# The root of the mixer's RMS norm, applied behind the input projections instead of in front of them

## The chip, the cores and the metric

One core of one Trainium2 chip runs the whole program. TensorE (PE) multiplies, VectorE (DVE), ScalarE (ACT) and GpSimd (Pool) do the elementwise work, and SyncE (SP) fetches weights. The metric is the device time of one execution in microseconds, as the median of several runs. Everything is float32: each matrix product is done as three products of split operands (high times high, low times high, high times low), so each activation tile needs a high part and a low part before PE can use it.

## The reference, cut to what matters

Two blocks run one after the other on 1024 tokens of width 1024. The first block ends in a layer norm. The second block begins with the lines below; what comes after them (the output projection, the feed-forward part, the gated embedding) is not touched.

```python
x = _layernorm(DN_ALPHA * x + y, ssd_ln_g, ssd_ln_b)      # end of the first block
h = x
a = rmsnorm(h, g_mix)                  # h * rsqrt(mean(h*h) + 1e-6) * g_mix
proj = a @ w_in
cb, cc, cu, q, k, v = split(proj)      # 512 columns each
v_ = cc * cu; y = causal 3-tap conv(v_) per channel; conv = cb * y; conv_out = head_rmsnorm(conv)
z = q . k * dh**-0.5                   # 8 heads of 64, stick-breaking attention
a_ij = exp(log_sigmoid(z_ij) + sum of log_sigmoid(-z) over the keys between j and i)
attn = a @ v; attn_out = head_rmsnorm(attn)
h = h + concat(conv_out, attn_out) @ w_out
```

The norm's root is one number per token. `a @ w_in` is linear, so the root of a token can be multiplied in behind the product.

## The kernel before, in words

Activations lie with the channels on the partitions: `H` is eight tiles k of 128 channels by 1024 tokens, `XH` and `XL` are the high and low parts of the eight tiles that the projections read. A weight slab is 128 output columns by all 1024 input channels; PE does it in eight pieces k, one for each tile, of six matmuls of 512 columns. SP fetches slabs into `w_stage`; Pool splits each into `w_hi` and `w_lo` (`split`, L612 and L615: one cast and four subtractions). `next_slab(n)` waits until slab n - 2 is done on PE, because two slots are there. A sum over the channels is a matmul with a matrix of ones (`CN`).

Each engine is one queue in program order, and its order is written out by hand; semaphores join the queues. Around the change the program runs as follows.

- PE does pieces of a small projection (`proj_piece`, L1243) between the norms' sums. `norm_sums` (L1036) adds up eight square tiles with 16 matmuls, once for the layer norm (`ln2`) and once for the mixer norm (`mix`). ACT makes the squares into two buffers `SQN` and waits for PE to have read the one before last.
- For the layer norm DVE makes `TN = H * gain * root` (L2531) and `H = TN + bias` (L2523) for the eight tiles, while ACT squares `TN + bias` (L1976). With the sums of these ACT makes the mixer's root. DVE then goes over the tiles a second time: `TN = H * g_mix * root` (L2531), ACT copies it to `XH` (L1762), and DVE makes `XL = TN - XH` (L2519).
- The input projection has 24 slabs in the order `SB_ORDER`: v0, q0, k0, cc0, cu0, v1, q1, k1, cb0, cc1, ... , cb3, in four rounds m of 128 channels (two heads). PE does the first two slabs interleaved: eight pieces of slab 0 with pieces of slab 1 between them, as tiles become ready (`mix["lo"]`). Then comes slab k0, the turning of v, and the attention.
- The attention goes in 12 steps a round, of up to 128 keys by 512 queries for two heads, over 10 blocks of keys in flight behind each other. `SB_FILL` sets how many pieces of later slabs PE does in each step. In a step PE makes scores (L1315), DVE copies them to `ZS` (L2874), ACT makes abs, exp and ln of it (L2060, L2072, L2074), DVE makes the softplus (L2905), ACT its high part (L2084), DVE its low part (L2907), PE the suffix sums (L1332), DVE subtracts them (L2889), ACT makes the weight (L2079) and its high part `WH` (L2089), DVE its low part `WL` (L2845), and PE multiplies with v (L1354).
- The convolution's channels go beside it: ACT copies cc into `CC` (L2008), DVE multiplies cu in (L2809), applies the three taps into `CONV` (L2822, L2825) and multiplies cb in (L2813).

## Time and profile before

| | |
|---|---|
| median of 3 runs | 2723.09 us (2722.91 to 2728.45) |
| the profiled execution | 2722.69 us, its span 2720.9 us |
| PE busy | 2642.7 us, 97% of the span |
| DVE, ACT, Pool busy | 1713.4, 938.1, 1150.4 us |
| granted PE clock | full in all 40 slices |
| first layer-norm tile scaled | at 1372.74 us |
| slabs 0 and 1 (v0, q0) done on PE | at about 1421.8 us |
| attention | 1436 to 1864 us |

Times are counted from the start of the span. A row of the timeline is: start, length, engine, line, operation, what is written from what is read, count, and in brackets how long the engine had been idle and what ended that. A matmul of 512 columns is shown with a modelled end, so its row is longer than its share of PE's time; the distance of two starts is the better measure. A row of the groups is: line, engine, operation, operands and sizes, count, then busy time, mean in ns, idle time before and its releasers. A row of a stretch is: its length, then busy time and count of PE, of the weight loads, of DVE, ACT and Pool, the granted clock, the share of the DMA engines and GB/s.

### The profile page before, as it was taken

To read this page: it belongs to the slowest core of one execution; us is meant where nothing else is said; L and a number is where in the kernel's file an instruction comes from. 1 tells how busy PE (TensorE), PEld (TensorE's weight loads), DVE (VectorE), ACT (ScalarE), POOL (GpSimd) and SP (SyncE) were. 2 spreads that over 40 slices of the span, in tenths; PEclk is the share of its full clock that TensorE was granted. 3 is DMA by queue.
4 is the path that set the end of the run, shared out by engine and by line. 5 is a ranking of instruction groups with operands and counts; after the bars stand their busy time and mean duration, and the time that the engine had idled before them with its cause. 6 is when DMAs were issued, how large, how long until landed. Compare 5 with 4: busy or idle time off the path is not lost.

```text
span 2720.9 us, 32191 instructions
## 1 busy us (share of the span) xinstructions
PE 2642.7 (97%) x12394; PEld 2117.3 (78%) x12394; DVE 1713.4 (63%) x2087; ACT 938.1 (34%) x1208; POOL 1150.4 (42%) x1422
## 2 busy tenths in 40 slices
PE   8999999999999999999999999998999999999998
PEld 7877878787887887887767777776888888888886
DVE  6636663778658658758865665666355656555556
ACT  2537880422212211212256666575211111111132
POOL 4633435431431431431421222223555676655653
PEclk9999999999999999999999999999999999999999
DMA  3110003210110110110230000002111111111312
GB/s 135 51 47 32 24 20 109 66 47 24 39 48 23 40 54 16 47 47 16 78 131 24 32 24 32 24 32 85 55 39 55 55 55 55 47 47 54 117 47 78
DMA packets 39937, 139.37 MB, mean 51 GB/s; under 512 B 4400, under 2 KB 4528, under 8 KB 39792
## 3 DMA queue, kind: packets, MB, share of 16 engines
q1 hardware_dynamic: 31392, 110.11, 12.3%
q10 hardware_dynamic: 8400, 27.26, 2.7%
q8 instruction: 99, 1.62, 0.3%
q14 instruction: 46, 0.38, 0.0%
HBM read 124.77 MB, written 12.58 MB: 50 GB/s over the span
## 4 chain that ended last, share of the span: by engine, by line
PE 82%; DVE 11%; ACT 4%; issue 2%; POOL 1%; ACTq 0%; DVEq 0%; POOLq 0%
PE PS L759 37%; PE PS L1437 13%; PE PS L1463 10%; PE PS L996 2%; PE PS L1089 2%; PE PS L1485 2%; PE PS L1130 2%; PE PS L1315 1%; PE PS L895 1%; PE PS L1332 1%; PE PS L909 1%; PE PS L1354 1%; PE PS L1132 1%; PE PS L1036 1%; ACT mla_p L1662 1%
## 5 line engine op out<-in xcount | busy, mean ns | idle before, releaser
L612 POOL CAST w_hi<-w_stage 128x1024 fp32r<-128x1024 f32 x130 | 143.3, 1102 | 1116.7 <-PE PS L759 757.9
L615 POOL TENSOR_TENSOR w_lo<-w_stage,w_hi 128x256 fp32r<-128x256 f32 x520 | 504.2, 1000 | 10.4
L759 PE MATMUL PS<-XH,w_hi 128*128 128x512 f32 x1216 | 384.6, 398 | 7.7 <-DVE XL L2519 2.9
L759 PE MATMUL PS<-XL,w_hi 128*128 128x512 f32 x1216 | 375.9, 390 | 0.0
L759 PE MATMUL PS<-XH,w_lo 128*128 128x512 f32 x1216 | 375.4, 390 | 0.0
L759 PEld LDWEIGHTS PS<-XH,w_hi 128*128 128x128 f32 x1216 | 222.4, 188 | 61.0 <-issue 10.0
L759 PEld LDWEIGHTS PS<-XL,w_hi 128*128 128x128 f32 x1216 | 228.4, 188 | 48.5
L759 PEld LDWEIGHTS PS<-XH,w_lo 128*128 128x128 f32 x1216 | 228.4, 188 | 48.4
L686 POOL TENSOR_TENSOR w_lo<-w_stage,w_hi 128x256 fp32r<-128x256 f32 x260 | 220.3, 854 | 0.0
L682 POOL CAST w_hi<-w_stage 128x256 fp32r<-128x256 f32 x260 | 125.9, 487 | 185.7 <-PE PS L1437 108.3
L1437 PE MATMUL PS<-raw_hi,w_hi 128*128 128x512 f32 x512 | 158.2, 390 | 0.0
L1437 PE MATMUL PS<-raw_hi,w_lo 128*128 128x512 f32 x512 | 157.8, 390 | 0.0
L1437 PE MATMUL PS<-raw_lo,w_hi 128*128 128x512 f32 x512 | 157.8, 389 | 0.0
L1463 PE MATMUL PS<-ffn_u_hi,w_lo 128*128 128x512 f32 x392 | 152.7, 390 | 0.0
L1463 PE MATMUL PS<-ffn_u_hi,w_hi 128*128 128x512 f32 x392 | 152.7, 390 | 0.0
L1463 PE MATMUL PS<-ffn_u_lo,w_hi 128*128 128x512 f32 x392 | 152.7, 389 | 0.0
L3009 DVE TENSOR_TENSOR H<-H,PS 128x512 f32<-128x512 f32 x140 | 96.0, 686 | 77.0 <-PE PS L1463 77.0
L2950 DVE SCALAR_TENSOR_TENSOR ffn_t<-PS,root 128x1024 f32<-128x1024 f32 x32 | 39.2, 1225 | 154.3 <-PE PS L1437 145.1
L2139 ACT ACTIVATE ffn_t<-ffn_t 128x1024 f32<-128x1024 f32 x32 | 34.0, 1061 | 240.0 <-DVE ffn_t L2950 240.0
L1437 PEld LDWEIGHTS PS<-raw_hi,w_hi 128*128 128x128 f32 x512 | 96.2, 188 | 20.2 <-issue 0.5
L1437 PEld LDWEIGHTS PS<-raw_lo,w_hi 128*128 128x128 f32 x512 | 96.2, 188 | 19.9
L1437 PEld LDWEIGHTS PS<-raw_hi,w_lo 128*128 128x128 f32 x512 | 96.2, 188 | 19.9
(459 smaller groups left out, 5620.7 us busy)
## 6 DMA issues: line engine op xcount, KB each, us to landing
w_stage<-w SPq DMA_DIRECT2D x202, 512.0 KB, 3.3
H<-x_t ACTq DMA_DIRECT2D x8, 512.0 KB, 8.0
pj_kept<-ple_proj_tiles ACTq DMA_DIRECT2D x8, 512.0 KB, 2.6
h_kept<-H ACTq DMA_DIRECT2D x8, 512.0 KB, 3.5
H<-h_kept ACTq DMA_DIRECT2D x4, 1024.0 KB, 5.0
out_t<-out_tiles SPq DMA_DIRECT2D x16, 256.0 KB, 2.1
x_again<-x_t ACTq DMA_DIRECT2D x12, 256.0 KB, 3.1
ple_proj_a<-pj_kept ACTq DMA_DIRECT2D x1, 2048.0 KB, 9.1
```

Source lines behind the costliest of these rows:

```text
L612: nc.gpsimd.tensor_copy(w_hi[:, slot, :, :], w_stage[:, slot, :, :]).then_inc(s_w_hi, 1)
L615: nc.gpsimd.tensor_tensor(w_lo[:, slot, k:k + 2, :], w_stage[:, slot, k:k + 2, :], w_hi[:, slot, k:k + 2, :].bitcast(F32), ALU.subtract).t ...
L682: nc.gpsimd.tensor_copy(ring(w_hi, e), src).then_inc(s_eh.sem, 1)
L686: nc.gpsimd.tensor_tensor(ring(w_lo, e), src, ring(w_hi, e).bitcast(F32), ALU.subtract).then_inc(done, count)
L759: mm = nc.tensor.matmul(outs[:, half, :], wt[:, slot, k, :], a[:, k - first, half * HB:(half + 1) * HB], start=(k == whole[0] and wt is w_ ...
L996: mm = nc.tensor.matmul(PS[:, 2 * (n % 2) + half, :], wt[:, n % 2, k, :], a[:, k, half_cols(half)], start=(k == 0 and wt is w_hi and a is ...
L1089: mm = nc.tensor.matmul(PS[:, half, :], wt[:, n % 2, k, :], a[:, k, half * HB:(half + 1) * HB], start=(k == 0 and wt is w_hi and a is XH), ...
L1130: nc.tensor.matmul(PS[:, 2, 64 * h:64 * h + 64], E[:, c % 2, h, :], XF[:, c % 2, 64 * h:64 * h + 64], start=True, stop=True)
L1437: mm = nc.tensor.matmul(PS[:, 2 * (c % 2) + half, :], ring(wt, e + k // 2, k % 2), a[:, k, half * HB:(half + 1) * HB], start=(k == 0 and w ...
L1463: mm = nc.tensor.matmul(PS[:, BANK[j], :], ring(wt, e + i, k), a[:, ACTS_AT[j], k, :], start=(j not in BEFORE and k == 0 and wt is w_hi an ...
L1485: mm = nc.tensor.matmul(PS[:, 4 + 2 * e + half, :], ring(wt, e0 + k // 2, k % 2), a[:, t, half * HB:(half + 1) * HB], start=(first and wt ...
L3009: v.tensor_tensor(dst, dst, src, ALU.add).then_inc(s_dr, 1)
```

## The change

What is done to the mixer norm:

- `XH` and `XL` are made from `H * g_mix`, with no root in them. `norm_two` takes the place of two calls of `norm_dve`: one pass in which DVE makes `TN`, then `H` (a tile later), then `XL` (two tiles later), and ACT makes the square and `XH` of each tile and issues the copy of `H` to `h_kept` behind it.
- PE's 16 matmuls over the squares are gone. The squares go into four buffers; Pool adds the first four tiles (`mix_add`, three additions around the split of slab 1), DVE the last four behind the last `XL`, and PE does two matmuls with ones over the sum, in the middle of slab k0.
- ACT makes the root `RM` (one number a token, on all partitions) while PE does the rest of k0. DVE makes from it `RK`, the same numbers with the tokens on the partitions (`key_roots`).
- The root comes in at four places. The score copy is `PS * RK * RM` (key's root and query's root). The weights' high and low parts are multiplied by `RK` (the root of v's token). Pool multiplies `CC` by `RM * RM` (cc and cu have one root each) and `CONV` by `RM` (for cb).
- PE's order of slabs 0 and 1 is `MIX_PIECES`: 0 0 0 1 1 0 1 0 1 0 1 0 1 0 1 1.

The diff, cut to its core:

```diff
+MIX_PIECES = [0, 0, 0, 1, 1, 0, 1, 0, 1, 0, 1, 0, 1, 0, 1, 1]
...
+            def mix_add(k):
+                mix["sq"].wait(pool, k + 1)
+                if k > 1:
+                    mix["ss"].wait(pool, k - 1)
+                nc.gpsimd.tensor_tensor(ACM[:, :], mix_square_at(0) if k == 1 else ACM[:, :], mix_square_at(k), ALU.add).then_inc(mix["ss"].sem, 1)
+            def root_squared():
+                mix["rs"].wait(pool, 1)
+                nc.gpsimd.tensor_tensor(RM2[:, :], RM[:, :], RM[:, :], ALU.mult).then_inc(mix["c"].sem, 1)
+            def gate_rooted(m):
+                pool.wait_ge(s_bank, sb_bank_turn(("cc", m)) + 1)
+                mix["c"].wait(pool, root_product("cc", m) - 1)
+                nc.gpsimd.tensor_tensor(CC[:, :], CC[:, :], RM2[:, :], ALU.mult).then_inc(mix["c"].sem, 1)
+            def taps_rooted(m):
+                pool.wait_ge(s_cc, cc_step("tap", m, 2))
+                nc.gpsimd.tensor_tensor(CONV[:, m, :], CONV[:, m, :], RM[:, :], ALU.mult).then_inc(mix["c"].sem, 1)
+            mix_add(1)
+            next_slab(N_IN2 + 1)
+            mix_add(2)
+            mix_add(3)
+            for i in range(2, len(SB_ORDER)):
+                next_slab(N_IN2 + i)
+                if i == 5:
+                    root_squared()
+                if SB_ORDER[i - 2][0] == "cc":
+                    gate_rooted(SB_ORDER[i - 2][1])
+                if SB_ORDER[i][0] == "cb" and i < len(SB_ORDER) - 1:
+                    taps_rooted(SB_ORDER[i][1])
+            next_slab(N_OUT2)
+            taps_rooted(3)
+            next_slab(N_OUT2 + 1)
...
-            norm_sums(mix)
...
+            for i in MIX_PIECES:
+                sb_piece(i, done[i])
+                done[i] += 1
+            progress[0] = 16
+            sb_pieces(4)
+            mix["ss"].wait(pe, KT - 1)
+            for half in range(2):
+                mm = nc.tensor.matmul(PS[:, 2 + half, :], CN[:, C_ONES, :], ACM[:, half * HB:(half + 1) * HB], start=True, stop=True)
+            mm.then_inc(mix["cs"].sem, 1)
+            sb_pieces(4)
...
-                        nc.scalar.activation(WH[:, T1 % 2, :, q1:HB], a, ACT.Copy).then_inc(s_wh, 1)
+                        nc.scalar.activation(WH[:, T1 % 2, :, q1:HB], a, ACT.Copy, scale=RK[:, j1:j1 + 1]).then_inc(s_wh, 1)
...
-            norm_dve(ln2, "ln2_g", center=centre2, split=False, keep=True)
-            norm_dve(mix, "g_mix")
+            norm_two(centre2)
...
-                v.tensor_tensor(WL[:, T % 3, :, q0:HB], ZS[:, T % 3, :, q0:HB], WH[:, T % 2, :, q0:HB].bitcast(F32),
-                                ALU.subtract).then_inc(s_wl, 1)
+                v.scalar_tensor_tensor(out=WL[:, T % 3, :, q0:HB], in0=ZS[:, T % 3, :, q0:HB], scalar=RK[:, j:j + 1],
+                                       in1=WH[:, T % 2, :, q0:HB].bitcast(F32), op0=ALU.mult, op1=ALU.subtract).then_inc(s_wl, 1)
...
-                        v.tensor_copy(z, PS[:, 0:2, q0:HB]).then_inc(s_zc, 1)
+                        v.scalar_tensor_tensor(out=z, in0=PS[:, 0:2, q0:HB], scalar=RK[:, j:j + 1],
+                                               in1=RM[:, hf * HB + q0:(hf + 1) * HB].unsqueeze(1).to_broadcast([P, 2, HB - q0]),
+                                               op0=ALU.mult, op1=ALU.mult).then_inc(s_zc, 1)
```

DVE's queue between the layer norm's last tiles and the end of the tile work. Before (L2531 scales, L2523 adds the bias, L2519 makes `XL`):

```order
L2531 SCALAR_TENSOR_TENSOR norm_t<-H,VC,norm_rs 128x1024
L2523 TENSOR_SCALAR H<-norm_t,VC 128x1024 x2
L2531 SCALAR_TENSOR_TENSOR norm_t<-H,VC,norm_rs 128x1024 x2
L2519 TENSOR_TENSOR XL<-norm_t,XH 128x1024
L2531 SCALAR_TENSOR_TENSOR norm_t<-H,VC,norm_rs 128x1024
```

Now (L2599 scales, L2593 adds the bias, L2588 makes `XL`, L2611 adds squares):

```order
L2599 SCALAR_TENSOR_TENSOR norm_t<-H,VC,norm_rs 128x1024
L2593 TENSOR_SCALAR H<-norm_t,VC 128x1024
L2588 SCALAR_TENSOR_TENSOR XL<-H,VC,XH 128x1024
L2593 TENSOR_SCALAR H<-norm_t,VC 128x1024
L2588 SCALAR_TENSOR_TENSOR XL<-H,VC,XH 128x1024 x2
L2611 TENSOR_TENSOR mix_square_sum<-mix_square_sum,norm_sq 128x1024 x2
L2611 TENSOR_TENSOR mix_square_sum<-mix_square_sum,mix_sq_b 128x1024 x2
```

The second pass over the tiles is gone, `XL` stands between the layer norm's own steps, and four additions stand behind the last `XL`.

Pool's queue around the split of slab 1 (the second cast of each piece). Before:

```order
L612 CAST w_hi<-w_stage 128x1024
L615 TENSOR_TENSOR w_lo<-w_stage,w_hi 128x256 x4
L612 CAST w_hi<-w_stage 128x1024
L615 TENSOR_TENSOR w_lo<-w_stage,w_hi 128x256 x4
L612 CAST w_hi<-w_stage 128x1024
```

Now:

```order
L649 TENSOR_TENSOR w_lo<-w_stage,w_hi 128x256 x4
L697 TENSOR_TENSOR mix_square_sum<-norm_sq 128x1024
L646 CAST w_hi<-w_stage 128x1024
L649 TENSOR_TENSOR w_lo<-w_stage,w_hi 128x256 x4
L697 TENSOR_TENSOR mix_square_sum<-mix_square_sum,mix_sq_b 128x1024 x2
L646 CAST w_hi<-w_stage 128x1024
```

One addition stands ahead of the split of slab 1 and two behind it, ahead of the split of k0.

Pool's queue at the split of slab v1 (the sixth of the input projection), where the first products with the root stand. Before there were casts and subtractions alone, as above; now:

```order
L649 TENSOR_TENSOR w_lo<-w_stage,w_hi 128x256 x4
L646 CAST w_hi<-w_stage 128x1024
L649 TENSOR_TENSOR w_lo<-w_stage,w_hi 128x256 x4
L701 TENSOR_TENSOR mix_root_squared<-mix_root 128x1024
L706 TENSOR_TENSOR conv_gated<-conv_gated,mix_root_squared 128x1024
L646 CAST w_hi<-w_stage 128x1024
```

Three more gates (L706) and four products of the taps (L710) follow in the same manner, each alone behind the split of a slab.

## Rows read from the trace of the kernel before

**Rows 1.** The page, busy time of each engine:

```profile
PE 2642.7 (97%) x12394; PEld 2117.3 (78%) x12394; DVE 1713.4 (63%) x2087; ACT 938.1 (34%) x1208; POOL 1150.4 (42%) x1422
```

**Rows 2.** Busy time by stretch: the mixer's squares, and slab 0's start:

```profile
1380.20:1390.20 10.00, 9.95 (x23) 4.45 (x24) 8.46 (x9) 6.57 (x6) 0.00 (x0) 1.00 0.84 337
...
1396.80:1403.70 6.90, 4.64 (x18) 3.23 (x18) 6.87 (x4) 4.09 (x4) 6.82 (x5) 1.00 0.38 152
```

**Rows 3.** Timeline of PE: the mixer's sums, slab 0's second piece, slab k0's first:

```profile
1380.25 10.57 PE L1036 MATMUL PS<-norm_sq,CN 128*128 128x512 f32 x24 [0.54 <-ACT norm_sq L1976]
...
1400.43 0.74 PE L759 MATMUL PS<-XH,w_hi 128*128 128x512 f32 x2 [1.93 <-DVE XL L2519]
...
1421.83 0.73 PE L759 MATMUL PS<-XH,w_hi 128*128 128x512 f32 x2
```

**Rows 4.** The chain that ended last, slabs 0 to 2:

```profile
1403.78 29.23 PE PS L759 x126
```

**Rows 5.** Groups of instructions from 1369.8 to 1421.8 us, PE, DVE and ACT:

```profile
L1036 PE MATMUL PS<-norm_sq,CN 128*128 128x512 f32 x34 | 15.5, 599 | 0.6 <-ACT norm_sq L1976 0.5
...
L2523 DVE TENSOR_SCALAR H<-norm_t,VC 128x1024 f32<-128x1024 f32 x8 | 5.9, 748 | 0.0
...
L1976 ACT ACTIVATE norm_sq<-norm_t,VC 128x1024 f32<-128x1024 f32 x8 | 9.1, 1148 | 5.1 <-PE PS L1036 2.2 <-DVE norm_t L2531 2.0 <-ACT ple_proj_tiles L1954 0.9
...
L1954 ACT ACTIVATE ple_proj_tiles<-PS 128x1024 f32<-128x1024 f32 x4 | 4.0, 1006 | 0.0
```

**Rows 6.** Timeline of DVE: scaling without Pool beside it, a split with it:

```profile
1372.74 2.48 DVE L2531 SCALAR_TENSOR_TENSOR norm_t<-H,VC,norm_rs 128x1024 f32<-128x1024 f32 x2 [8.97 <-ACT norm_rs L1542]
...
1382.28 1.28 DVE L2531 SCALAR_TENSOR_TENSOR norm_t<-H,VC,norm_rs 128x1024 f32<-128x1024 f32 x1
...
1398.64 1.74 DVE L2519 TENSOR_TENSOR XL<-norm_t,XH 128x1024 fp32r<-128x1024 f32 x1
```

**Rows 7.** Timeline of Pool: the splits of slabs 1 and 2:

```profile
1396.34 1.30 POOL L612 CAST w_hi<-w_stage 128x1024 fp32r<-128x1024 f32 x1 [31.98 <-PE PS L1243]
1397.72 6.60 POOL L615 TENSOR_TENSOR w_lo<-w_stage,w_hi 128x256 fp32r<-128x256 f32 x4
1417.83 1.04 POOL L612 CAST w_hi<-w_stage 128x1024 fp32r<-128x1024 f32 x1 [13.52 <-PE PS L759]
1418.95 2.83 POOL L615 TENSOR_TENSOR w_lo<-w_stage,w_hi 128x256 fp32r<-128x256 f32 x4
```

**Rows 8.** Groups of instructions of Pool, all: its operation on 1024 columns:

```profile
L633 POOL TENSOR_TENSOR XL<-H,XH 128x1024 fp32r<-128x1024 f32 x7 | 16.5, 2370 | 0.0
```

**Rows 9.** Groups by shape, the replaced operations (in the attention) and their like:

```profile
L2874 DVE COPY sb_z<-PS 128x1024 f32<-128x1024 f32 x24 | 29.2, 1218 | 0.1
...
L2551 DVE SCALAR_TENSOR_TENSOR ssd_conv<-PS,VC,ssd_conv 128x1023 f32<-128x1023 f32 x24 | 30.8, 1283 | 0.8
...
L2089 ACT ACTIVATE sb_weight_hi<-sb_z 128x1024 fp32r<-128x1024 f32 x24 | 25.1, 1046 | 0.1
...
L1915 ACT ACTIVATE ssd_y_hi<-ssd_conv,VC 128x1024 fp32r<-128x1024 f32 x12 | 13.8, 1154 | 11.9 <-DVE ssd_conv L2690 11.9
```

**Rows 10.** Waits, 1436 to 1863 us (waiter, releaser, total us, times, longest):

```profile
PEld PS L1354 <- DVE sb_weight_lo L2845: 15.7, 24, 2.0
...
PEld PS L1332 <- DVE sb_softplus_lo L2907: 9.8, 10, 1.5
```

**Rows 11.** Timeline of Pool, DVE and PE at slab cb0's split:

```profile
1519.29 3.87 POOL L615 TENSOR_TENSOR w_lo<-w_stage,w_hi 128x256 fp32r<-128x256 f32 x4
...
1523.69 1.23 DVE L2907 TENSOR_TENSOR sb_softplus_lo<-sb_softplus,sb_softplus_hi 128x1024 fp32r<-128x1024 f32 x1 [1.13 <-ACT sb_softplus_hi L2084]
...
1524.97 0.74 PE L1332 MATMUL PS<-sb_softplus_hi,from_r 128*128 128x512 f32 x2 [0.68 <-DVE sb_softplus_lo L2907]
```

**Rows 12.** Timeline of Pool and DVE at the end of the attention:

```profile
1854.79 1.64 POOL L612 CAST w_hi<-w_stage 128x1024 fp32r<-128x1024 f32 x1 [25.86 <-PE PS L759]
...
1855.45 2.06 DVE L2845 TENSOR_TENSOR sb_weight_lo<-sb_z,sb_weight_hi 128x1024 fp32r<-128x1024 f32 x1
```

## What the change does to the time, predicted from these rows

> **What bounds the kernel now.** I read the page first. PE is busy for 97% of the span [rows 1], so time is won only where PE waits or does work that can go. The busy time by stretch and PE's timeline show where that is around the mixer's norm. The 16 matmuls of its sums stand in the trace as two rows each; 24 rows take 10.57 us, or 0.44 each [rows 3], so the sums alone take PE 14 us, in which it is full and DVE is busy for 8.46 of 10 us [rows 2]. When slab 0 begins, PE is busy for 4.64 us of 6.9, since DVE makes each `XL` out of two steps and shares its time with Pool [rows 2]; PE's longest wait there is 1.93 us [rows 3]. Behind that, PE runs without a gap: 126 matmuls in 29.23 us, or 1.39 us for a piece of six [rows 4]. Slab k0 starts at 1421.83 us [rows 3]. That moment is the gauge of the first half of the change. The second half lies in the attention, where PE's weight loads wait for the weights' low part in 24 of 48 steps and for the softplus' low part in 10 [rows 10]. So there DVE is the late one in up to half of the steps, and what is added to it costs something.
>
> The sum is made against the profiled execution of 2722.7 us; the median, 2723.1, is 0.4 more.
>
> **The norm's stretch: when does k0 start?** Up to the first scaled tile at 1372.74 us nothing changes [rows 6]. From there DVE has for each tile a scaling of 1.28 us, a bias step of 0.75 and an `XL` of about 1.28 (it now has a gain too, like the scaling) [rows 5, 6]: 3.31 us, and 26.5 for eight. Alone it would have the last `XL` at 1399.2. ACT has less to do: eight squares of 1.15, eight `XH` of 1.15 (an ACT copy with a gain takes that [rows 9]) and four copies of 1.01 are 22.4 us [rows 5]; it sets no end.
>
> Pool lies beside this with the split of slab 1 and three additions. What a Pool operation costs DVE can be read in one place for a short one: beside Pool's quarters of the split an `XL` took 1.74 us instead of some 1.25 [rows 6], so a quarter costs 0.5. Pool pays too: the split took 1.30 and 6.60 us with DVE beside it and 1.04 and 2.83 alone [rows 7]. For a cast on 1024 columns it is more: it began at 1854.79 and lasted 1.64, and the DVE subtraction that began at 1855.45 behind it took 2.06 us, 0.84 too long [rows 12]. It looks as if each waits for the other to end. The slab's split then costs DVE 0.7 + 4 x 0.5 = 2.7 us. An addition on 1024 columns takes Pool 2.37 us [rows 8]; no row shows one beside a DVE operation that reads two tiles of SBUF. Its price is between 0.45, as for a quarter, and 2.1, nearly its whole length. I take 1.5, since the cast is nearest in size and held DVE for most of its own length: 4.5 us for three. The last `XL` is then at 1399.2 + 2.7 + 4.5 = 1406.4.
>
> The Trainium skill (SBUF — State Buffer, section on SBUF's two separate sides) states that the loser of the pair of ports that VectorE and GpSimd share "fully blocks", for the whole instruction, when the VectorE instruction has two SBUF inputs. Rows 12 agree for a cast; no row shows a two-input Pool operation of 2.37 us. By that rule an addition here would cost about 2.1, by the rule of the short row 0.45; the first would move the whole sum to slower, the second to faster, and each is a rival below.
>
> PE needs eight pieces of slab 0 and eight of slab 1, and has a few waiting when the last `XL` comes; I put the end of slab 0 at 1409. Only then may Pool split k0. DVE's four additions (4.9 us at 1.22) run then, so the split takes some 5 us, between 3.9 alone and 7.9 [rows 7], where before it was hidden behind slab 1. k0 starts at 1414: **7.8 us earlier**. PE idles for 2 us before it; the two pieces of slab 1 left are no cover for the split. The bounds are 1410 (additions at 0.45, last `XL` at 1403.3) and 1416 (at 2.1, last `XL` at 1408.2, and PE, starved on the way, ends slab 0 at 1411.5).
>
> **The two matmuls over the sum** are four such rows of 0.44 us: **+1.8**. The 16 that go give PE nothing of their own here: DVE's walk above sets k0's start, and it has left them out. The squares are all added by then. The root's logarithm and exponential, `key_roots` on DVE and one more table load run beside the second half of k0, 5.5 us, and its turning; they cost nothing unless the root is over 3 us late. The copies to `h_kept` and the projection's last pieces move with ACT and are not waited for.
>
> **Arithmetic in the attention.** The score copy goes from 1.218 to 1.283 us, what DVE takes from PSUM with a tile and a column [rows 9]; the weights' low part gains a column too, +0.06; its high part on ACT goes from 1.046 to 1.154 [rows 9]. That is 0.23 us a step. If all 48 steps paid it, it would be 11 us; if only the 24 that wait for the weights paid, and half of them absorbed it in the order of the queues, some 1.5. Lower bound nothing. I take **+1.5**: the chain that ended last goes through PE in most of the attention.
>
> **Pool's nine products in the attention.** The split of cb0 ends at 1523.16; the softplus' low part starts at 1523.69, and PE already waits for it 0.68 us [rows 11]. The product for y starts between the two and takes 2.37 [rows 8], so it can hold DVE for up to 1.85, straight onto PE. The same pattern stands in rounds 1 and 2. At slab cc0 two products follow each other in steps that wait for DVE: up to 2. At the end of the last round the last product starts with the taps, and the split and the cast chain of rows 12 move behind it: up to 1.5. The gates of cc1 to cc3 fall where PE has 18 matmuls to go on with; I cost them nothing, and up to 1 together where that cover is short. At most that makes 3 x 1.85 + 2 + 1.5 + 1 = 10; at 0.45 apiece, five on the path, 2.3. I take 1.2 for each of the three, 1.2 and 0.7: **+5.5**. cu and cb wait for Pool's products too, but these are done a slab earlier, except cb3's, which ends at about the time its slab does.
>
> **Sum:** -7.8 + 1.8 + 1.5 + 5.5 = +1.0, so 2723.7 against the profiled execution and 2724.1 against the median. I forecast **2724.1 us**, no change that can be measured.
>
> **Rivals.**
>
> - *Pool's long operations cost DVE no more than short ones.* k0 starts at 1410, -11.8; +1.8, +1.5, +2.3: -6.2, or 2716.9. For it: nothing in the trace shows a long hold by a two-input operation. Against it: the cast of rows 12.
> - *Each Pool operation holds DVE for its whole length* (the rule above). k0 starts at 1416, -5.8; +1.8, +1.5, +10: +7.5, or 2730.6. It decides from a hold of about 1.9 us where PE already waits for the softplus' low part. For it: rows 11 and 12. Against it: Pool may start just after DVE, and then Pool is the one that waits.
> - *The attention is covered by PE's slabs*: neither the arithmetic nor the products reach PE, and only the norm's gain is left, -7.8 + 1.8 = -6.0, or 2717.1. Against it: 34 waits of rows 10.
> - *The longer steps of the attention all reach PE*: -7.8 + 1.8 + 11 + 5.5 = +10.5, or 2733.6. Against it: the chain goes mostly through PE.
>
> **How the numbers follow.** The forecast's own range is 2718 to 2728.5, with a chance of 0.50. The first rival gets 0.16, the third 0.09, the second 0.18 and the fourth 0.07. A difference of 0.2%, 5.4 us, is about what a measurement of this kernel can tell from no change. Faster by more: the two faster cases, 0.25, and 0.02 out of the forecast's tail; slower by more: the two slower ones, 0.25; the rest, 0.48. The range that should hold it 8 times in 10 reaches over both signs: 2713 to 2733. It leaves out the faster cases' better halves and what lies beyond the fourth rival's lower half.
>
> **What would show each step.** In the profile after: the start of the first matmul of k0 (1410, 1414 or 1416); the time of the last `XL` and the length of a DVE step beside a Pool addition (1.7 or 3.3); the idle time of PE before k0, by Pool's `w_lo`; the length of the score copy (1.28) and of `WH` (1.15); and in the attention the length of the softplus' low part in the step behind each product for y (1.23, or up to 3.1), with PE's wait behind it. From k0's start to the end of the attention (1864) 442 us pass before; the forecast adds 9 to it. More than 13 added would make it wrong on the slow side, less than 4 on the fast side.

## The result, and the profile after

| | before | after |
|---|---|---|
| median | 2725.43 us (6 runs, 2722.91 to 2730.12) | 2735.75 us (6 runs, 2734.27 to 2737.16) |
| ratio | | 1.0037, 95% interval 1.0027 to 1.0047 |
| profiled execution, its span | 2722.69, 2720.9 us | 2734.27, 2732.4 us |
| mean granted clock of it | 0.998 | 0.993 |

The change makes the kernel 10.3 us slower. The forecast was 2724.1 with a range to 2733; the time lies above both.

Busy times of the page after, to set beside [rows 1]: PE has no more work than before, and it is idle for 90.9 us of its span where it was idle for 78.2.

```profile
PE 2641.5 (97%) x12366; PEld 2116.9 (77%) x12366; DVE 1737.2 (64%) x2085; ACT 942.4 (34%) x1208; POOL 1181.1 (43%) x1434
```

The first scaled tile comes at 1372.74 us in the trace of before and at 1373.95 in the trace after; in the other kernels' traces it lies anywhere from 1372.4 to 1377.9, in code that is the same in all. So all offsets below are counted from that first scaled tile: `k0` is the start of slab k0, `att` the first scores, `end` the last head sums, each against the same moment of before (49.1, 63.8 and 497.8 us after the first scaled tile).

| after, against before | k0 | att | step 4 | round 1 | round 2 | round 3 | end |
|---|---|---|---|---|---|---|---|
| us | -6.3 | -3.0 | -0.3 | +1.6 | +5.3 | +7.9 | +10.1 |

**The norm's stretch.** DVE's timeline of after, then Pool's. Two scalings that fall beside a Pool addition take 3.42 and 3.38 us where they take 1.28 alone, and a bias step (0.75 in [rows 5]) takes 2.89.

```profile
1380.19 3.42 DVE L2599 SCALAR_TENSOR_TENSOR norm_t<-H,VC,norm_rs 128x1024 f32<-128x1024 f32 x1
...
1391.14 3.38 DVE L2599 SCALAR_TENSOR_TENSOR norm_t<-H,VC,norm_rs 128x1024 f32<-128x1024 f32 x1
1394.44 2.89 DVE L2593 TENSOR_SCALAR H<-norm_t,VC 128x1024 f32<-128x1024 f32 x1
...
1406.75 1.28 DVE L2588 SCALAR_TENSOR_TENSOR XL<-H,VC,XH 128x1024 fp32r<-128x1024 f32 x1 [0.25 <-ACT XH L2054]
```

```profile
1379.49 3.04 POOL L697 TENSOR_TENSOR mix_square_sum<-norm_sq 128x1024 f32<-128x1024 f32 x1 [13.92 <-ACT norm_sq L2050]
...
1390.09 6.69 POOL L697 TENSOR_TENSOR mix_square_sum<-mix_square_sum,mix_sq_b 128x1024 f32<-128x1024 f32 x2
1411.90 1.04 POOL L646 CAST w_hi<-w_stage 128x1024 fp32r<-128x1024 f32 x1 [15.12 <-PE PS L828]
1413.02 3.64 POOL L649 TENSOR_TENSOR w_lo<-w_stage,w_hi 128x256 fp32r<-128x256 f32 x4
```

PE's timeline of after, in slab 0 and at the start of k0, and the stretches around them (the granted clock is the third number from the end of a row of a stretch). Two matmuls of a product start 0.45 us before the next two at full clock (the forecast's 1.39 us for six); here they are 0.85 apart, and the granted clock is 0.72 and 0.79, where it was 1.00 throughout before. Between its two levels, 2.4 and 1.2 GHz, PE ran at the lower one for a few us, each time behind a wait of about 2 us.

```profile
1391.27 1.22 PE L828 MATMUL PS<-XH,w_hi 128*128 128x512 f32 x2 [1.96 <-DVE XL L2588]
1392.29 1.06 PE L828 MATMUL PS<-XL,w_hi 128*128 128x512 f32 x2
1393.14 1.06 PE L828 MATMUL PS<-XH,w_lo 128*128 128x512 f32 x2
...
1416.72 0.73 PE L828 MATMUL PS<-XH,w_hi 128*128 128x512 f32 x2 [2.17 <-POOL w_lo L649]
...
1418.37 1.06 PE L828 MATMUL PS<-XH,w_hi 128*128 128x512 f32 x2
1419.22 1.06 PE L828 MATMUL PS<-XL,w_hi 128*128 128x512 f32 x2
...
1423.94 1.88 PE L1452 MATMUL PS<-mix_square_sum,CN 128*128 128x512 f32 x4
```

```profile
1383.20:1395.40 12.20, 8.21 (x25) 5.78 (x24) 12.20 (x8) 5.40 (x6) 11.71 (x7) 0.72 0.59 217
...
1416.70:1424.70 8.00, 7.98 (x26) 6.16 (x27) 0.28 (x1) 0.21 (x1) 3.73 (x5) 0.79 0.40 131
```

**The attention.** The place of [rows 11], now with the product of the taps in it: the softplus' low part takes 2.88 us where it took 1.23, and PE waits 2.34 us for it where it waited 0.68. A round later a wait of 2.33 us at the same step is followed by pairs 0.85 to 1.02 us apart, so at the lower clock. It is the only one of the three such waits (2.34, 2.33 and 2.33 us, in rounds 0 to 2) at which the clock fell.

```profile
1524.24 2.37 POOL L710 TENSOR_TENSOR conv_out<-conv_out,mix_root 128x1024 f32<-128x1024 f32 x1
...
1524.81 2.88 DVE L3000 TENSOR_TENSOR sb_softplus_lo<-sb_softplus,sb_softplus_hi 128x1024 fp32r<-128x1024 f32 x1 [1.13 <-ACT sb_softplus_hi L2156]
...
1527.75 0.74 PE L1400 MATMUL PS<-sb_softplus_hi,from_r 128*128 128x512 f32 x2 [2.34 <-DVE sb_softplus_lo L3000]
...
1643.41 1.22 PE L1400 MATMUL PS<-sb_softplus_hi,from_r 128*128 128x512 f32 x2 [2.33 <-DVE sb_softplus_lo L3000]
1644.43 1.05 PE L1400 MATMUL PS<-sb_softplus_lo,from_r 128*128 128x512 f32 x2
```

The groups by shape and the waits of the attention in the trace after answer to [rows 9] and [rows 10]. The longer steps have the forecast's sizes; the wait for the softplus' low part has grown from 9.8 us in 10 waits to 15.5 in 9, that for the weights' from 15.7 to 20.4.

```profile
L2965 DVE SCALAR_TENSOR_TENSOR sb_z<-PS,SM,mix_root 128x1024 f32<-128x1024 f32 x24 | 30.7, 1278 | 0.1
L2162 ACT ACTIVATE sb_weight_hi<-sb_z,SM 128x1024 fp32r<-128x1024 f32 x24 | 27.3, 1139 | 0.1
```

```profile
PEld PS L1422 <- DVE sb_weight_lo L2934: 20.4, 24, 2.1
PEld PS L1400 <- DVE sb_softplus_lo L3000: 15.5, 9, 2.8
```

### The profile page after: what moved, and what is told of

Same layout as the page of the kernel before. It is cut to its first block, busy times and chain, and to the rows that moved or that the text cites. A ratio compares the mean times of both kernels' runs of the same rounds, so it can differ in the third digit from the quotient of the medians.

```text
span 2732.4 us, 32159 instructions
## 1 busy us (share of the span) xinstructions
PE 2641.5 (97%) x12366; PEld 2116.9 (77%) x12366; DVE 1737.2 (64%) x2085; ACT 942.4 (34%) x1208; POOL 1181.1 (43%) x1434
## 4 chain that ended last, share of the span: by engine, by line
PE 79%; DVE 13%; ACT 4%; issue 3%; POOL 1%; ACTq 0%; DVEq 0%; POOLq 0%
PE PS L828 35%; PE PS L1511 13%; PE PS L1537 10%; PE PS L1065 2%; PE PS L1158 2%; PE PS L1559 2%; PE PS L1199 2%; PE PS L964 1%; PE PS L978 1%; PE PS L1383 1%; PE PS L1201 1%; PE PS L1422 1%; PE PS L1400 1%; DVE ssd_x L2685 1%; ACT mla_p L1736 1%
## 5 line engine op out<-in xcount | busy, mean ns | idle before, releaser
L1511 PEld LDWEIGHTS PS<-raw_hi,w_hi 128*128 128x128 f32 x512 | 96.1, 188 | 20.4 <-issue 0.5
```

What stands on the lines that cost most here:

```text
L1511: mm = nc.tensor.matmul(PS[:, 2 * (c % 2) + half, :], ring(wt, e + k // 2, k % 2), a[:, k, half * HB:(half + 1) * HB], start=(k == 0 and w ...
```

## The experiments

All were run beside the kernel before; its median was 2725.16 us for the first four, 2725.28 for the next four, 2725.09 for the three after them and 2725.85 for the last. The offsets are those of the profiled execution, counted as above. The clock is the mean granted clock of all timed runs of a kernel (before: 0.996). The ratio and its interval are taken over the timed runs and are not the quotient of the two medians; where the runs of a kernel scatter widely, as in f1, e4 and g3, the two differ by up to 0.0009. Runs of one kernel scatter by several us, so a difference of less than about 3 us between two medians is not clear of noise.

| kernel | median, us | ratio to before, 95% | clock | k0 | att | end |
|---|---|---|---|---|---|---|
| the change | 2735.75 | 1.0037 (1.0027 to 1.0047) | 0.9922 | -6.3 | -3.0 | +10.1 |
| e1 tiny products | 2725.68 | 1.0001 (0.9991 to 1.001) | 0.9939 | -6.4 | -3.0 | +2.6 |
| e2 norm alone | 2722.48 | 0.9991 (0.9981 to 1.0) | 0.9940 | -6.3 | -3.0 | -3.4 |
| e3 products in quarters | 2727.92 | 1.0007 (0.9998 to 1.0017) | 0.9938 | -6.4 | -3.0 | +3.4 |
| e4 tiny additions | 2731.79 | 1.0016 (1.0007 to 1.0026) | 0.9924 | -12.7 | -9.4 | +6.8 |
| f1 no y product | 2726.05 | 1.001 (1.0001 to 1.002) | 0.9938 | -6.3 | -3.0 | +3.3 |
| f2 additions on DVE | 2735.63 | 1.0038 (1.0026 to 1.0049) | 0.9919 | -9.3 | -5.9 | +7.7 |
| f3 filler before k0 | 2736.76 | 1.004 (1.0026 to 1.0054) | 0.9910 | -6.4 | -4.7 | +11.0 |
| f4 all on DVE | 2722.47 | 0.9989 (0.9979 to 0.9998) | 0.9942 | -9.3 | -7.6 | -5.7 |
| g1 y product later | 2730.11 | 1.0016 (1.0007 to 1.0025) | 0.9923 | -6.4 | -4.6 | +5.1 |
| g2 v root once | 2725.08 | 0.9996 (0.9987 to 1.0005) | 0.9952 | -9.3 | -5.9 | -2.2 |
| g3 plain scores | 2724.69 | 0.999 (0.9981 to 0.9999) | 0.9946 | -9.3 | -5.9 | +0.4 |
| h1 v root first | 2720.33 | 0.9979 (0.997 to 0.9988) | 0.9948 | -9.0 | -5.6 | -4.4 |

### Which part costs: the products, the arithmetic, the additions

e1 makes Pool's nine products one column wide:

```diff
-                nc.gpsimd.tensor_tensor(CC[:, :], CC[:, :], RM2[:, :], ALU.mult).then_inc(mix["c"].sem, 1)
+                nc.gpsimd.tensor_tensor(CC[:, 0:1], CC[:, 0:1], RM2[:, 0:1], ALU.mult).then_inc(mix["c"].sem, 1)
```

> The changed kernel, but Pool's nine products with the root (its square, four gates of cc, four products of the taps) work on 1 column of 1024, so the convolution's root is left out; all waits stay. Theory H (a long Pool operation holds every DVE operation that reads two tiles of SBUF for its whole length, and PE's clock falls in the gap): of the 12.9 us that the attention lost in the changed kernel some 11 come back, 2735.8 to about 2725, the step behind each split of cb goes back from 2.88 to 1.23 us for the softplus' low part. Theory A (the longer arithmetic, 0.23 us in 48 steps): these products matter little, 2734 or more.

Measured: 2725.68, 10.1 us less than the change. The products cost nearly twice the forecast's 5.5, and they are the whole loss. It is not a kinder clock that did it: in the two profiled executions, between the first scaled tile and the last head sums, the granted clock of e1 is 0.97 and that of the change 0.98, and e1 is still 7.5 us ahead at the end.

e2 does the same and also takes the roots out of the score copy and the weights' two parts, so that only the norm's stretch is changed:

```diff
-                        nc.scalar.activation(WH[:, T1 % 2, :, q1:HB], a, ACT.Copy, scale=RK[:, j1:j1 + 1]).then_inc(s_wh, 1)
+                        nc.scalar.activation(WH[:, T1 % 2, :, q1:HB], a, ACT.Copy).then_inc(s_wh, 1)
```

> As the kernel with one-column products, and the score copy and the weights' high and low parts as in the kernel before, without the root: what is left of the change is the norm's stretch alone. Theory H: at most 1 us less than the kernel with one-column products, and 2 to 4 us faster than the kernel before, since slab k0 starts some 5 us earlier and two matmuls and a stretch at half clock take 3 of them back. Theory A: some 8 us less than with one-column products.

Measured: 2722.48, 2.7 us under before, and 3.2 under e1, which has the arithmetic in addition. Its offset stays at -3.0 us through all 48 steps: what the norm's stretch wins reaches the end, and nothing else is touched.

e3 keeps the products and cuts each into four of 256 columns:

```diff
+                for q in range(4):
+                    s_ = slice(q * P * 2, (q + 1) * P * 2)
+                    ins = nc.gpsimd.tensor_tensor(out_[:, s_], a[:, s_], b[:, s_], ALU.mult)
```

> The changed kernel with each of Pool's nine products as four operations on 256 columns. Theory H: a hold ends with the operation, 0.6 us, and DVE comes in between, so the softplus' low part behind y's product falls from 2.88 to below 2 us; PE's gaps there stay under 1.5 us and its clock stays up: 4 to 6 us faster than the changed kernel. If instead the hold goes by Pool's whole queue, or DVE is slowed by Pool's total work, it is no faster than the changed kernel.

Measured: 2727.92, 7.8 us less than the change with all of the work still there, and more than the 4 to 6 expected. Pool's and DVE's timelines at the place of [rows 11] show why. The low part is not held at all now (1.25 us), the step behind it by 0.5, and Pool takes twice its time: between two quarters DVE gets in.

```profile
1527.29 4.78 POOL L702 TENSOR_TENSOR conv_out<-conv_out,mix_root 128x256 f32<-128x256 f32 x4
...
1527.85 1.25 DVE L3006 TENSOR_TENSOR sb_softplus_lo<-sb_softplus,sb_softplus_hi 128x1024 fp32r<-128x1024 f32 x1 [1.13 <-ACT sb_softplus_hi L2162]
1529.03 1.75 DVE L2940 SCALAR_TENSOR_TENSOR sb_weight_lo<-sb_z,SM,sb_weight_hi 128x1024 fp32r<-128x1024 f32 x1
```

e4 makes the three additions on Pool one column wide instead, and DVE's first one adds the square of tile 4 to itself, so that the squares of tiles 0 to 3 are left out of the sum:

```diff
-nc.gpsimd.tensor_tensor(ACM[:, :], mix_square_at(0) if k == 1 else ACM[:, :], mix_square_at(k), ALU.add).then_inc(mix["ss"].sem, 1)
+nc.gpsimd.tensor_tensor(ACM[:, 0:1], (mix_square_at(0) if k == 1 else ACM[:, :])[:, 0:1], mix_square_at(k)[:, 0:1], ALU.add).then_inc(mix["ss"].sem, 1)
```

> The changed kernel with Pool's three additions of squares on 1 column of 1024, and DVE's first addition from one square twice, so the mean leaves out the first four tiles; waits and DVE's work as before. Theory H: each addition held DVE by about 2 us, so the last XL comes 6 us earlier, slab k0 starts 5 to 7 us earlier and the gaps that lowered PE's clock there shrink: 5 to 7 us faster than the changed kernel. Theory A: no difference.

Measured: k0 starts 6.4 us earlier than in the change, 3 x 2.1, the lengthening of three DVE steps, so the hold is whole there too. But the time falls by 4.0 only: the offset goes from -9.4 at the first scores to -3.4 at the end of round 0. f2, f3 and g1 below lose 3 to 6 us in that round too.

### Is it the place, or the work?

f1 leaves out the four products of the taps (`taps_rooted`) and DVE's wait for them. The head norm divides by the root of the same token again, so only its eps is met otherwise.

```diff
-                if SB_ORDER[i][0] == "cb" and i < len(SB_ORDER) - 1:
-                    taps_rooted(SB_ORDER[i][1])
...
-                    mix["c"].wait(dve, root_product("y", m))
```

> The four products of the taps with the root are left out (the head norm behind them divides by the root of the same token, so only its eps is met otherwise); the root squared and the four gates stay on Pool. The tiny products took 10 us off the changed kernel. Theory H (a Pool operation holds the softplus' low part for its whole length where PE already waits): the y products stand at such places, the gates do not, so leaving four of nine out gives back 6 to 7 of the 10: 2729 (2728 to 2730). Rival N (the products cost by their number, wherever they stand, through DVE's total): four ninths of 10, so 2731.3. By H the softplus' low part behind each y product is back at 1.23 us and PE's wait before it under 1 us.

Measured: 2726.05, 9.7 us less than the change (8.2 by the means of the runs, where e1 has 10.2; 6.8 and 7.5 at the end of the profiled executions). Four of the nine products carry nearly all of the loss that the nine make; with the root squared and the gates gone as well (e1) no further gain is clear of the scatter. Theory H was right about the place and too mild about the size. The trace of f1 still has the 2.7 us of the step at which the root squared and the first gate stand, where e1 has nothing and loses 3.0 us between steps 6 and 10 instead, at and behind the drop of its clock that is shown below.

g1 leaves the product as it is and lets it start 1.8 us or so later, behind the low part that it stood beside:

```diff
             def taps_rooted(m):
                 pool.wait_ge(s_cc, cc_step("tap", m, 2))
+                if m < 3:
+                    pool.wait_ge(s_spl, NU * (m + 1))
```

> The changed kernel with one wait more: in rounds 0 to 2 Pool starts the product of the taps with the root only when DVE has finished the last softplus' low part of the round, beside which it stood; the product itself is the same, and its result is needed some 30 us later. Theory P (the place decides: held is the one step for which PE waits): the jumps of 1.7, 2.9 and 1.8 us at the starts of rounds 1 to 3 go or become small, the low part takes 1.23 us again, and the time is 2730.5 (2729 to 2732). Rival A (a Pool operation of this length costs the same wherever it stands beside DVE): 2735.7.

Measured: 2730.11, 5.6 us less than the change, at the same work and even a lower clock than in e1. The place decides. The jumps at the starts of rounds 1 to 3 are 0.0, 0.0 and 0.1 us (1.7, 2.9 and 1.8 in the change). DVE's and Pool's timelines of g1:

```profile
1528.63 1.23 DVE L3002 TENSOR_TENSOR sb_softplus_lo<-sb_softplus,sb_softplus_hi 128x1024 fp32r<-128x1024 f32 x1 [1.13 <-ACT sb_softplus_hi L2158]
1529.78 1.28 DVE L2936 SCALAR_TENSOR_TENSOR sb_weight_lo<-sb_z,SM,sb_weight_hi 128x1024 fp32r<-128x1024 f32 x1
1531.15 1.22 DVE L2984 TENSOR_TENSOR sb_z<-sb_z,PS 128x1024 f32<-128x1024 f32 x1
...
1530.00 3.31 POOL L712 TENSOR_TENSOR conv_out<-conv_out,mix_root 128x1024 f32<-128x1024 f32 x1 [1.90 <-DVE sb_softplus_lo L3002]
```

DVE has begun the weights' low part 0.22 us before Pool begins, and now Pool is the one that waits: 3.31 us instead of 2.37, DVE 1.28 as ever. And the subtraction behind it, which reads PSUM, runs beside Pool's product in its usual 1.22 us.

The Trainium skill (SBUF — State Buffer, section on SBUF's two separate sides) says just this: of the two the one that starts first has the shared ports for the whole instruction, and it names DVE instructions with two SBUF inputs, and those in a 2-port mode, as the ones concerned. The traces agree for steps with two SBUF tiles (2.88 for 1.23 us), for the free step on PSUM, and for the bias step with one SBUF tile (2.89 for 0.75), if its 0.75 us for 1024 columns is such a mode.

### Where Pool's additions go

f2 lets DVE do the three additions, each behind an `XL`:

```diff
                     if k > 1:
                         low(k - 2)
+                    if 4 <= k <= 6:
+                        squares_added(k - 3)
```

> The three additions of squares that Pool did are done by DVE, one behind each of the XL of tiles 2, 3 and 4 of the one pass; nothing else is changed. By the changed kernel's rows each Pool addition lengthens a DVE step by 2.1 us (3.42 for 1.28, 3.38 for 1.28, 2.89 for 0.75), 6.3 together; three additions on DVE cost 3 x 1.22 = 3.7. Theory H: k0 starts 2.7 us earlier, counted from the first scaled tile, and the time is 2733.1 (2732 to 2734.5). Rival S (k0's start is set by the split of its slab beside DVE's last additions, not by the last XL): no gain, 2735.7. Rival L (the shared time is small): k0 1 us later or more, 2737.

Measured: k0 starts 3.0 us earlier than in the change, as theory H had it (2.7), so rival S is wrong about k0. But the time is 2735.63, no gain. In the profiled execution 2.4 us of the earlier start are left at the end (+7.7 for +10.1); in the timed runs nothing is, at a lower mean clock than any kernel here but f3. The gain is made and given back.

### The clock

f3 puts two matmuls nobody reads into the gap before k0:

```diff
             progress[0] = 16
+            pe.wait_ge(s_pj, 8)
+            for half in range(2):
+                nc.tensor.matmul(PS[:, 2 + half, :], CN[:, C_ONES, :], CN[:, 0:4, :].rearrange("p a t -> p (a t)"), start=True, stop=True)
```

> Two matmuls with ones over constants, whose result nobody reads, stand on PE in the gap of 2.17 us before slab k0 (1.88 us of work); all else is the changed kernel. Theory C (the granted clock falls to half because PE stood idle): the stretch behind k0's start is at full clock, its first three pieces take 1.39 us each instead of 1.65, 2.56 and 1.62, so k0's slab ends some 1.7 us earlier counted from its start, and the time is 2734.0. Rival X (the clock falls there for another reason, such as the load before): the granted clock of the stretch stays under 1 and the time is 2735.7.

Measured: behind k0's start the granted clock is 1.00, and the first scores come 1.7 us earlier than in the change, as theory C had it. Yet the time is 2736.76, no better: by step 5 the offset is -1.2, against -0.5 in the change, with a clock of 0.92 between 1436 and 1480 us (0.96 in the change). The rows of stretches of f3, then those of f4 (below) behind its k0:

```profile
1419.30:1427.30 8.00, 7.92 (x31) 5.93 (x32) 0.34 (x1) 0.72 (x2) 3.83 (x6) 1.00 0.39 133
1436.00:1480.00 44.00, 38.19 (x200) 29.98 (x200) 27.12 (x34) 27.35 (x41) 11.73 (x11) 0.92 0.08 24
```

```profile
1416.30:1424.30 8.00, 7.89 (x31) 5.88 (x32) 0.37 (x1) 0.70 (x2) 3.85 (x6) 1.00 0.40 133
```

f4 has no filler; up to k0 its program is that of f2, k0 starts at the same distance from the first scaled tile (39.8 us), behind the same wait of 2.17 us. f2 then has the half clock (its granted clock is 0.79 from 1412 to 1420 us), and f4 has not. So a wait of 2 us is an occasion for the clock to fall, but the same wait does not always do it. e1 and e2 show it in the attention too, at the same values step of round 0 behind the same wait; PE's timeline of e1 and of e2:

```profile
1502.85 1.22 PE L1422 MATMUL PS<-sb_weight_hi,sb_v_hi_lo 128*128 128x512 f32 x2 [1.59 <-DVE sb_weight_lo L2934]
1503.87 1.05 PE L1422 MATMUL PS<-sb_weight_lo,sb_v_hi_lo 128*128 128x512 f32 x2
```

```profile
1500.35 0.73 PE L1422 MATMUL PS<-sb_weight_hi,sb_v_hi_lo 128*128 128x512 f32 x2 [1.58 <-DVE sb_weight_lo L2934]
1500.92 0.63 PE L1422 MATMUL PS<-sb_weight_lo,sb_v_hi_lo 128*128 128x512 f32 x2
```

How much of a difference is clock can be estimated from the timed runs, since the clock differs between runs of one kernel. Before alone ran from a span of 2720.5 us at 0.998 to 2729.2 at 0.993. Over all 220 runs, each against the mean of its kernel in its own set of runs, 0.001 less clock goes with 1.67 us more. Taken with that slope (it says what goes together, not what causes what), the mean spans split so:

| against before, us | all | with the clock | the rest |
|---|---|---|---|
| the change | +10.1 | +6.2 | +3.9 |
| e1 tiny products | 0.0 | +3.3 | -3.4 |
| e2 norm alone | -3.0 | +3.2 | -6.2 |
| f4 all on DVE | -2.8 | +2.8 | -5.7 |
| h1 v root first | -5.7 | +1.8 | -7.5 |

### Versions that put it right

f4 takes everything of the mixer norm off Pool: additions as in f2, no product of the taps as in f1, ACT squares the root, and DVE takes cc out of PSUM times it, in place of ACT's copy and Pool's gate.

```diff
-                    nc.scalar.activation(CC[:, :], flat(3), ACT.Copy).then_inc(s_bank, 1)
+                    v.tensor_tensor(CC[:, :], flat(3), RM2[:, :], ALU.mult).then_inc(s_bank, 1)
```

> Nothing of the mixer norm is left on Pool: DVE adds all squares, ACT squares the root while it waits for slab k0, DVE takes cc from PSUM times the squared root in place of ACT's copy and Pool's gate, and the products of the taps are left out (they cancel in the head norm but for its eps). Theory H: the 10 us of the products go (-10), DVE's additions give 2.7, four DVE steps of 1.28 us in place of ACT's copies cost 0 to 5, I take 2: 2735.7 - 10 - 2.7 + 2 = 2725.0 (2723 to 2728). Rival D (DVE is so late in the attention that each step more on it costs PE its whole length): +5, 2728. If Pool has nothing to do with the loss the time stays above 2732.

Measured: 2722.47, 2.5 us under the expectation and just under its range; the four DVE steps cost nothing that shows.

g2 and g3 ask for the arithmetic. g2 multiplies v's root in once a round, into the turned v, and takes it out of the weights; g3 has the plain score copy in addition (the roots of key and query are left out).

```diff
+            def v_rooted(m):
+                dve.wait_ge(s_vt, m + 1)
+                v.tensor_tensor(VT[:, :].rearrange("p (j t) -> p j t", t=P), PS[:, 2:4, :].rearrange("p b (x d) -> p (b x) d", d=P),
+                                RK.unsqueeze(2).to_broadcast([P, KT, P]), ALU.mult).then_inc(mix["c"].sem, 1)
```

> The version that has nothing on Pool, and in it the root of v's token is no longer multiplied into the weights' high and low parts of all 48 steps, but once a round into the turned v (one DVE step of 1.28 us a round, four in all, in a stretch in which DVE waits 2 us or more), from which the high and low parts of v are then made. Theory W (the arithmetic in the steps costs what the runs with and without it differ by, 3.2 us, and half of that lies in the weights): 1.6 us less than 2722.5, so 2720.9 (2719.5 to 2722). Rival E (only the score copy's 0.06 us a step counts, since it is the first of the chain of a step): 2722.5. Rival V (the v step is waited for at each round's start): up to 4 x 1.3 more, 2727.

> As the version with the root of v's token multiplied in once a round, and the score copy is the plain copy of before, so the roots of key and query are left out of the scores. It shows the floor of the change, with no arithmetic left in the 48 steps. Theory W: another 1.6 us less, 2719.3 (2718 to 2721). Rival E: the whole 3.2 us lie here, 2719.3 too, but 3.2 under the version with the roots. Rival Z (the arithmetic costs nothing, the difference seen was the scatter): no difference between the two.

Measured: 2725.08 and 2724.69. Rival V's mechanism holds: each of three round starts costs g2 and g3 1.5 or 1.6 us. The step stands behind `add_parts`, which waits for ACT, and it pushes k's low part back, for which PE waits 1.47 us (PE's timeline of g2). Between g2 and g3 the medians differ by 0.4 us, which cannot be told from nothing and is what rival Z had. It does not show that the score copy's roots are free: g3 ran at the lower mean clock (0.9946 for 0.9952), and the means of the runs are 1.2 us apart.

```profile
1535.79 0.33 PE L1354 MATMUL PS<-sb_q_hi,sb_k_hi 64*128 64x128 f32 x2 [1.47 <-DVE sb_k_lo L2869]
```

h1 puts the step ahead of `add_parts`:

```diff
+                    if step == NU + 1 and m < 3:
+                        v_rooted(m + 1)
                     if step == NU + 1:
                         add_parts(m, 1)
                     if step == NU + 1 and m < 3:
-                        v_rooted(m + 1)
                         v_lo(m + 1)
```

> As the version in which v's root is multiplied in once a round, but DVE does that step ahead of adding the attention's output parts, where it stood idle for 4 us, instead of behind it, so that v's low part and k's low part behind it are no later than in the version with the root in the weights. By the trace of the run before, PE waited 1.47 us for k's low part at each of three round starts, and each round start cost 1.3 to 1.5. Theory V: these 4.2 us go, and the weights' arithmetic stays away: 2725.1 - 4.2 = 2720.9 (2719 to 2723), the best version. Rival F (the clock gives the time away again elsewhere, as it did with the gain of the earlier start): 2722.5 to 2725.

Measured: 2720.33, ratio 0.9979 (0.997 to 0.9988): 4.8 us less than g2, and less than both the kernel before, by 5.5 us, and the change. DVE's timeline shows the step in what was idle time, and k's low part directly behind v's:

```profile
1535.97 1.22 DVE L2902 TENSOR_TENSOR sb_v_t<-PS,SM 128x1024 f32<-128x1024 f32 x1 [3.70 <-PE PS L1343]
1537.22 1.40 DVE L2917 TENSOR_TENSOR attn_out<-PS,sb_out_low_part 64x512 f32<-64x512 f32 x2
1538.65 1.23 DVE L2907 TENSOR_TENSOR sb_v_hi_lo<-sb_v_t,sb_v_hi_lo 128x1024 fp32r<-128x1024 f32 x1
1539.79 1.22 DVE L2869 TENSOR_TENSOR sb_k_lo<-PS,sb_k_hi 128x1024 fp32r<-128x1024 f32 x1
```

The three round starts cost 0.0 us each. Of the earlier start 1.5 us are lost in round 0 (-5.3 to -3.8), where the granted clock is 0.83 from 1500 to 1510 us.

## Why the prediction was wrong, point by point

- **The norm's walk: the time of the last `XL` came out by luck, and the last link was short.** The last `XL` ends at 1408.0 us, or 1406.8 with the trace's late start taken off; the forecast had 1406.4. Two errors cancel in that. The three Pool additions held DVE for 6.4 us, 2.1 each, the upper bound, where the forecast had 4.5; and DVE's own 24 steps took some 24.8 us where it had 26.5, since the three steps of a tile start 3.05 us apart and not 3.31. The split of slab 1 cost 2.6, as forecast (2.7). Slab 0 then ended at 1411.9 (1410.7 with the late start off) instead of 1409, since PE, starved and at half clock on the way, had pieces left to do, so k0's gain was 6.3 and not 7.8 us, nearer the second rival's 5.8 and for its reason.
- **The ones matmuls:** 1.7 us, forecast 1.8: from k0's start to the first scores f4, at full clock, takes 16.4 us where before takes 14.7 (the row of 1.88 has the modelled end in it). The root was hidden, as said.
- **The arithmetic: the steps right, their price too low.** The copies took 1.278 and 1.139 us (forecast 1.283 and 1.154). The forecast's own rule, 24 waiting steps of which half absorb 0.23 us, gives 2.8 us and not the 1.5 that it wrote. e1 and e2 differ by 3.2 us in the median, 3.0 in the mean, of which part is scatter. In their traces 3.1 of the 6.0 us by which they differ at the end come in round 0, most of them at and behind the clock drop shown above; rounds 1 and 2 add 0.6 and 0.5. g2 against g3 shows nothing clear of noise for the score copy. The rival that made all steps pay 11 us is out.
- **Pool's nine products: the term that failed.** The forecast had +5.5, with 1.2 for each y product, between 0.45 and 1.85. e1 puts the nine at 10.1 and f1 the four y products at 9.7. In the trace of the change the three round starts behind a y product cost 1.7, 2.9 and 1.8 us (the clock fell at the second), and the step of the root squared and the first gate 2.7, where the forecast had 1.2. The mechanism was the second rival's: Pool starts 0.6 us before DVE, and DVE's step grows by 1.65 us. The argument against it, that Pool might start just after DVE, could have been decided from the rows, and the prediction's own reading of them, that the product starts between the two, goes against it: the split of cb0 ended at 1523.16 and DVE's step began at 1523.69 [rows 11], and Pool's queue has nothing between the two. g1 shows that the other order would indeed have been free.
- **The clock: missing from the sum.** In the profile of before the granted clock is full in all 40 slices, and I took every microsecond of PE's work at full clock. In the trace of the change it fell, from the first scaled tile on, in slab 0, behind k0's start (1.6 us between there and the first scores), behind the waits of 1.55 and 1.80 us of the first gate's step, behind one of the three waits of 2.3 us, and at the end of the attention. By the slope above some 6 of the 10 us go with the clock; with the clock taken out the change stands at +3.9, against the forecast's +1.0 and the second rival's +7.5. This share is estimated from what goes together and no run shows it by itself: e1, without the loss, has the lower clock in its profiled execution.
- **The sign of being wrong** that the prediction gave, more than 13 us added from k0's start to the end of the attention, was there: 16.4 us, where the forecast had 9.
- **The range** ended at 2733, since the second rival's 2730.6 was its upper case. Its own bound of 10 for the products plus anything for the clock would have carried it past 2735.

What stays open is what makes the clock fall behind one wait of 2 us and not behind the next. f2 and f4 have the same program up to there and differ; f3 kept the clock up at one place and the time was lost further on. No run separates chance from a cause here.

## What to carry to other kernels

Work moved onto an idle Pool is not free for DVE: beside a DVE step on two SBUF tiles, whichever begins first holds the other for its whole length, so look up in the trace which DVE step begins while the Pool operation runs, and whether PE waits for it. If it does, cut the operation, start it behind that step, or let DVE read the operand from PSUM, as the steps that did so here kept their usual 1.22 us beside Pool. Where PE is the bound and runs at full clock, a wait that the change lengthens can cost more than its length (it did so behind some of the waits here and not behind others), so bound the sum with the clock at its lower level for a few microseconds behind each such wait.

## What the runs showed of the hardware

- A Pool operation of 2.37 us beside a DVE step of 1.23 made it 2.88 when Pool began 0.57 us ahead; when DVE began 0.22 us ahead, DVE took 1.28 and Pool 3.31. Four Pool operations of 256 columns beside two DVE steps took 4.78 us, and DVE 1.25 and 1.75.
- A DVE step of one SBUF tile that takes 0.75 us for 1024 columns was held too (2.89 us); steps that read PSUM were not (1.22 us).
- At half clock (1.2 GHz) two matmuls of 512 columns take 0.85 us, at full clock 0.45. Runs of one kernel differ by up to 10 us in span, and the mean granted clock goes with it: 1.67 us for 0.001.
